# Attention of a fused two-block kernel: where a head pair's projections and sums of squares stand among its steps

## The reference, cut to what matters

```python
q = (rms_norm_2(q_lat, q_a_g) @ w_q_b).reshape(bsz, L, MLA_HEADS, MLA_QK)
kv = (rms_norm_2(kv_lat, kv_a_g) @ w_kv_b).reshape(bsz, L, MLA_HEADS, MLA_NOPE + MLA_V)
k_nope, v = jnp.split(kv, [MLA_NOPE], axis=-1)
k = jnp.concatenate([k_nope, jnp.broadcast_to(k_pe[:, :, None, :], (bsz, L, MLA_HEADS, MLA_ROPE))], axis=-1)
q = rms_norm_2(q, q_norm_g)
k = rms_norm_2(k, k_norm_g)
q = jnp.concatenate([q[..., :MLA_NOPE], apply_rope(q[..., MLA_NOPE:], cos, sin)], axis=-1)
k = jnp.concatenate([k[..., :MLA_NOPE], apply_rope(k[..., MLA_NOPE:], cos, sin)], axis=-1)
...
    sc = jnp.einsum('bqhd,bkhd->bhqk', q[:, s:e], k[:, :e]).astype(jnp.float32) * scale
    mask = jnp.arange(e)[None, :] <= jnp.arange(s, e)[:, None]
    p = jax.nn.softmax(jnp.where(mask, sc, -jnp.inf), axis=-1).astype(v.dtype)
    outs.append(jnp.einsum('bhqk,bkhd->bqhd', p, v[:, :e]))
o = jnp.concatenate(outs, axis=1).reshape(bsz, L, MLA_HEADS * MLA_V)
return o @ w_out
```

## Time and profile before

| | us |
|---|---|
| median of 3 runs | 2866.23 |
| lowest and highest run | 2855.94, 2868.21 |
| profiled execution, its own time | 2863.25 |
| its span | 2861.4 |
| TensorE busy in the span | 2715.2 (95%) |
| the eight pairs' steps | 2138.0 to 2460.0 |

### The profile page before, as it was taken

How to read it: one execution, slowest core, us unless ns; L and a number is a source line. 1 busy time by engine, 2 the same in 40 slices (tenths; PEclk the granted TensorE clock), 3 DMA queues, 4 the chain that set the end, 5 groups by cost and what they waited for, 6 DMA issues and landing times.

```text
span 2861.4 us, 35969 instructions
## 1 busy us (share of the span) xinstructions
PE 2715.2 (95%) x15144; PEld 2310.3 (81%) x15144; DVE 1189.6 (42%) x1641; ACT 976.4 (34%) x1479; POOL 925.5 (32%) x381
## 2 busy tenths in 40 slices
PE   6999999899999987999999999999979999999999
PEld 4777778677777777999888999999957777778887
DVE  6444441444444237666666331112344444421111
ACT  3333333323333333444334332223333333433222
POOL 3343344333434432222222333444320000244443
PEclk9999999999999998999999999999976677999999
DMA  3233333222333221211121222332210000133332
GB/s 122 90 107 90 100 98 89 75 91 83 113 91 98 91 74 45 60 54 59 52 59 53 76 87 90 89 92 87 77 52 8 15 8 15 60 94 92 94 96 89
DMA packets 61328, 215.65 MB, mean 75 GB/s; under 512 B 8176, under 2 KB 8560, under 8 KB 61168
## 3 DMA queue, kind: packets, MB, share of 16 engines
q1 hardware_dynamic: 57248, 202.05, 23.5%
q10 hardware_dynamic: 3920, 11.31, 1.2%
HBM read 211.24 MB, written 2.10 MB: 75 GB/s over the span
## 4 chain that ended last, share of the span: by engine, by line
PE 89%; DVE 6%; ACT 2%; issue 2%; DMA 0%; POOL 0%; SPq 0%; ACTq 0%; DVEq 0%
PE psum L357 73%; PE psum L954 1%; PE psum L892 1%; PE psum L920 1%; PE psum L451 1%; PE psum L461 1%; PE psum L896 1%; PE psum L644 1%; PE psum L918 1%; PE psum L956 1%; PE psum L647 1%; PE psum L937 1%; PE psum L599 1%; PE psum L369 1%; PE psum L658 0%
## 5 line engine op out<-in xcount | busy, mean ns | idle before, releaser
L337 POOL TENSOR_TENSOR sb_w_lo<-sb_w_raw,sb_w_hi 128x1024 fp32r<-128x1024 f32 x377 | 925.3, 2457 | 1913.8 <-ACT sb_w_hi L1070 1913.6
L357 PE MATMUL psum<-sb_h_hi,sb_w_hi 128*128 128x512 f32 (+1 forms) x2648 | 827.6, 354 | 48.0 <-DVE sb_h_lo L1510 33.9
L357 PE MATMUL psum<-sb_h_lo,sb_w_hi 128*128 128x512 f32 (+1 forms) x2648 | 799.6, 344 | 0.0
L357 PE MATMUL psum<-sb_h_hi,sb_w_lo 128*128 128x512 f32 (+1 forms) x2648 | 796.3, 343 | 0.0
L1070 ACT ACTIVATE sb_w_hi<-sb_w_raw 128x1024 fp32r<-128x1024 f32 x377 | 395.5, 1054 | 612.3 <-PE psum L357 461.6
L357 PEld LDWEIGHTS psum<-sb_h_hi,sb_w_hi 128*128 128x128 f32 x2648 | 464.7, 193 | 120.1 <-issue 39.9
L357 PEld LDWEIGHTS psum<-sb_h_lo,sb_w_hi 128*128 128x128 f32 x2648 | 463.0, 192 | 62.8 <-issue 7.6
L357 PEld LDWEIGHTS psum<-sb_h_hi,sb_w_lo 128*128 128x128 f32 x2648 | 462.2, 192 | 56.1
L357 PE MATMUL psum<-sb_mix_hi,sb_w_hi 128*128 128x264 f32 (+1 forms) x1424 | 418.3, 339 | 11.5 <-DVE sb_mix_lo L2224 5.8
L357 PE MATMUL psum<-sb_mix_lo,sb_w_hi 128*128 128x264 f32 (+1 forms) x1424 | 416.0, 338 | 0.0
L357 PE MATMUL psum<-sb_mix_hi,sb_w_lo 128*128 128x264 f32 (+1 forms) x1424 | 414.1, 337 | 0.0
(11 more groups left out here) (269 smaller groups left out, 2671.9 us busy)
## 6 DMA issues: line engine op xcount, KB each, us to landing
sb_w_raw<-in_weights SPq DMA_DIRECT2D x377, 512.0 KB, 3.6
sb_decay<-in_decay ACTq DMA_DIRECT2D x16, 640.0 KB, 3.8
sb_resid<-in_x SPq DMA_DIRECT2D x4, 512.0 KB, 9.1
out<-sb_resid SPq DMA_DIRECT2D x8, 256.0 KB, 2.1
sb_table<-in_rope_table ACTq DMA_DIRECT2D x1, 264.0 KB, 3.6
sb_s<-in_positions ACTq DMA_DIRECT2D x1, 256.0 KB, 8.8
sb_cols<-in_cols ACTq DMA_DIRECT2D x1, 158.5 KB, 4.3
sb_ones<-in_ones ACTq DMA_DIRECT2D x1, 64.0 KB, 5.6
```

The costliest lines, as they stand in the source:

```text
L337: e.tensor_tensor(g.w_lo[:, u % 4, :], g.w_raw[:, u % 2, :], g.w_hi[:, u % 4, :].bitcast(F32), ALU.subtract).then_inc(S["w_lo"], 1)
L357: mm = e.matmul(g.psum[0:m, at + b, 0:wd], w[:, slot, P * i:P * i + m], xs[:, tile, c:c + wd], start=first and n == 0, stop=last and n == 2)
```

## The change

- **Blocks.** `pe_pair_block` issues one block. Block 0 goes behind step 2, block 1 between scores and transpositions of step 4, and two blocks each into steps 5, 6 and 7, one ahead of the transpositions and one at the end.
- **Sums.** `pe_pair_totals` is cut into halves of a head and uses banks 2 and 3 alone: half 0 behind step 1, the next inside step 2, the other head's two inside and behind step 3. The second head waits until `dve_pair_mean` has read the first.
- **VectorE.** The second turn part goes to step 1 and the third to step 2, the mean comes in two halves (steps 2 and 3), Newton moves to steps 5, 5 and 6, the key products to steps 6 and 7; the finished pair's output to step 4; `dve_finish` goes behind the other pair work of its step.
- **ScalarE.** The square of the queries goes ahead of the exponential of step 7, the reciprocal root to step 4, the split to step 2, the output copy to step 3. A first split of the output projection moves from behind the steps into the last pair.
- **TensorE, other.** `pe_out_turn` goes from step 4 to step 2. The output projection's fillers stand singly at 21 places in the last two pairs, in units 0, 1 and 2; seven blocks of unit 3 take the place of seven of unit 2 behind the steps, then come four last blocks (they were three), then units 4 to 7 (they were 3 to 7).

The number of instructions of each kind stays the same, but for one more mean per pair at half the size.

```diff
+PAIR_BLOCKS = tuple((3 * h + n, n, h, n == 0, n == 2) for h in range(2) for n in range(3))
+PAIR_BLOCKS += ((6, 3, 2, True, False), (7, 4, 2, False, True))
+def pe_pair_block(g, e, pair, i):
+    u = U_PAIRS[pair]
+    if i == 0:
+        e.wait_ge(S["lat_lo"], 5)
+        e.wait_ge(S["w_lo"], u + 1)
+        if pair:
+            e.wait_ge(S["q_squared"], pair)
+            e.wait_ge(S["turn"], 2 * pair + 2)
+    if i == 3 and pair >= 3:
         e.wait_ge(S["mix3"], pair - 2)
+    if i == 6 and pair:
+        e.wait_ge(S["mean"], rs_qk(pair - 1))
...
+def pe_pair_totals(g, e, pair, h, half):
+    if half == 0:
+        if h == 0:
+            e.wait_ge(S["q_squared"], pair + 1)
+            e.wait_ge(S["k_squared"], pair + 1)
+        else:
+            e.wait_ge(S["qk_mean"], pair + 1)
...
+    bank = 2 + half
...
-MLA_BANKS = (0, 2, 4, 5)
-FILL = {ALL_STEPS - 11: [(0, range(0, 3))], ALL_STEPS - 10: [(0, range(3, 6))],
-        ALL_STEPS - 7: [(1, range(0, 2))], ALL_STEPS - 6: [(1, range(2, 6))],
-        ALL_STEPS - 2: [(0, range(6, 7)), (1, range(6, 7))]}
+MLA_BANKS = (0, 2, 3, 4, 5, 0, 2, 3)
+FILLERS = [(m, n) for m in range(3) for n in range(PAIRS - 2)] + [(m, PAIRS - 2) for m in range(3)]
+PLACES = [(NS * (PAIRS - 2) + n, at) for n, at in ((2, 1), (4, 0), (5, 0), (5, 1), (6, 0), (6, 1), (7, 0), (7, 1))]
+PLACES += [(NS * (PAIRS - 1) + n, at) for n in range(1, NS) for at in range(2) if (n, at) != (4, 1)]
...
         pe_scores(g, e, i)
+        if more and n == 2:
+            pe_pair_totals(g, e, pair + 1, 0, 1)
+        if more and n == 3:
+            pe_pair_totals(g, e, pair + 1, 1, 0)
+        if project and n >= 4:
+            pe_pair_block(g, e, pair + 2, (1, 2, 4, 6)[n - 4])
...
         if i >= 1:
             pe_turn_p(g, e, i - 1)
         if i >= 2:
             pe_times_v(g, e, i - 2)
-        if pair + 1 < PAIRS:
-            if n == 1:
-                pe_pair_totals(g, e, pair + 1, 0)
-            if n == 2:
-                pe_pair_totals(g, e, pair + 1, 1)
-        if pair and n == 4:
+        if more and n == 1:
+            pe_pair_totals(g, e, pair + 1, 0, 0)
+        if more and n == 3:
+            pe_pair_totals(g, e, pair + 1, 1, 1)
+        if project and n == 2:
+            pe_pair_block(g, e, pair + 2, 0)
+        if pair and n == 2:
             pe_out_turn(g, e, pair - 1)
-        if pair + 2 < PAIRS:
-            if n == 5:
-                pe_pair_queries(g, e, pair + 2, 0)
-            if n == 6:
-                pe_pair_queries(g, e, pair + 2, 1)
-                pe_pair_keys(g, e, pair + 2)
+        if project and n >= 5:
+            pe_pair_block(g, e, pair + 2, (3, 5, 7)[n - 5])
...
+    pe_mla_out(g, e, 3, range(0, 3))
     pe_times_v(g, e, ALL_STEPS - 1)
-    pe_mla_out(g, e, 2, range(0, 7))
+    pe_mla_out(g, e, 3, range(3, 7))
     pe_out_turn(g, e, PAIRS - 1)
...
+    for m in range(4):
+        pe_mla_out(g, e, m, range(7, 8))
+    for m in range(4, KT):
         pe_mla_out(g, e, m, range(8))
```

More of the change, by code:

```diff
@@ L964, in pe_out_turn @@
     if pair + 2 < PAIRS:
-        e.wait_ge(S["mean"], rs_qk(pair + 2))
+        e.wait_ge(S["turn"], 2 * (pair + 2) + 4)
     if pair:
@@ L1004, in pe_mla @@
     pe_v(g, e, 0)
-    pe_pair_queries(g, e, 0, 0)
-    pe_pair_queries(g, e, 0, 1)
-    pe_pair_keys(g, e, 0)
+    for k in range(8):
+        pe_pair_block(g, e, 0, k)
     pe_v(g, e, 1)
[L1009 to L1013, removed]
+    for h in range(2):
+        for half in range(2):
+            pe_pair_totals(g, e, 0, h, half)
+    for k in range(8):
+        pe_pair_block(g, e, 1, k)
     for i in range(ALL_STEPS):
         pair, n = divmod(i, NS)
+        more, project = pair + 1 < PAIRS, pair + 2 < PAIRS
         pe_scores(g, e, i)
+        if more and n == 2:
[4 more added lines that the diff above has]
+            pe_pair_block(g, e, pair + 2, (1, 2, 4, 6)[n - 4])
+        if (i, 0) in FILL:
+            m, k = FILL[i, 0]
+            pe_mla_out(g, e, m, [k])
         if i >= 1:
@@ L1364, in act_pair_q_squares @@
     if pair:
-        e.wait_ge(S["qk_total"], pair)
+        e.wait_ge(S["qk_total"], 2 * pair)
     e.activation(g.square[0:QK, :, 0:SEQ], g.psum[0:QK, 0:2, :],
@@ L1423, in act_mla @@
     act_split(g, e, U_PAIRS[1] + LEAD)
-    act_rsqrt(g, e, rs_qk(0), g.mean2[:, :], g.rinv2[0][:, :])
+    act_pair_rsqrt(g, e, 0)
     act_pair_q_squares(g, e, 1)
-    act_pair_keys(g, e, 1)
     for i in range(ALL_STEPS):
         pair, n = divmod(i, NS)
+        if pair + 2 < PAIRS and n == 7:
+            act_pair_q_squares(g, e, pair + 2)
         act_exp(g, e, i)
@@ L2121, in dve_pair_plain @@
     S = g.S
-    e.wait_ge(S["q_proj"], pair + 1)
     e.wait_ge(S["q_squared"], pair + 1)
@@ L2177, in dve_pair_newton, with dve_pair_keys @@
         e.scalar_tensor_tensor(y, t, 1.5, y, ALU.add, ALU.mult).then_inc(S["newton"], 1)
-def dve_pair_keys(g, e, pair):
+def dve_pair_keys(g, e, pair, part):
     S = g.S
@@ L2240, in dve_mla @@
         dve_top(g, e, i)
-        if n == 1 and pair:
-            dve_finish(g, e, pair - 1, 1)
-        if n == 5:
-            dve_finish(g, e, pair, 0)
-        if n == 6 and pair:
-            dve_pair_out(g, e, pair - 1)
         if pair + 1 < PAIRS:
```

140 lines of the change are left out of this document (73 added, 67 removed).

## The result

The changed kernel takes 2823.55 us, the median of four runs (2832.88, 2814.31, 2814.26, 2832.78), beside 2867.22 us for the kernel before in the same session. The ratio is 0.9849, with a 95% interval of 0.9817 to 0.9881: 1.5% faster. The forecast was 2855.0, with a range that began at 2826, so the change was faster, as forecast, and by three and a half times as much (43.7 us against 12 from the same median; the two profiled executions, 2863.25 and 2832.88, differ by 30.4 us where the prediction's sum is 8.2).

A forecast was written before the change was run, and what follows sets the result against it. TensorE's own work at two clock prices was taken as the bound, waits as the smaller part. Terms -11.4 - 4.2 + 4.5 + 0.4 - 2.4 + 3.3 + 1.6 = -8.2 us, from 2863.25 to 2855; range 2826 to 2880.

The forecast's parts named there:

- The bound and the prices: Pairs' steps: TensorE's own work bounds; 28.2 us a pair at full clock, plus 0.447 us per microsecond at half clock.
- The waits: TensorE's waits for other engines in pairs 1 to 6: from 2.5 to 0.6 us a pair, -11.4 us.
- The new wait behind the squares of the keys: First sums of a pair would wait for ScalarE's late key copy and square: 0.2 to 0.6 us a pair.
- The half clock: Pairs 1 to 6: time at the lower clock falls from 27.5 to 26 us a pair, -4.2 us for six.
- the three places where the clock might return: Within a pair: step 3, step 4 or step 7, after 19, 19 or 35 us, weighed 0.4, 0.2, 0.4.
- Rival 3: Clock returns only in step 7 without the run of blocks: 36 us at half clock a pair, 2887 us; chance 0.16.
- Rival 1's middle case: Spread blocks keep work dense, clock up for longer: 15 us at half clock in each pair, 2825 us; chance 0.14.
- The sums let it fall: Steps 1 to 3: the sums' thin work brings the clock down, some 5.5 us of full-clock work into the pair.
- Pair 0: First pair: half clock grows from 17 to 27 us, +4.5 us.
- The ends: Last pair's idle time 3.0 to 0.6 us, -2.4; behind the steps, wait ahead of unit 4 +3.3, clock fall +1.6.
- The page on the clock: Skill page's rule: removing idle gaps would keep the clock up; the prediction said the trace disagrees, TensorE being busy throughout.

The follow-up runs named there:

- e1: Changed kernel with its eight blocks put back to three behind step 5 and five behind step 6: 2873.94 us, ratio 1.0024 to before.
- e2: Changed kernel with 16 useless matmuls added per pair around the sums of squares in steps 1 to 3: 2804.21 us, ratio 0.9788 to before.
- f1: Changed kernel with blocks 0 to 2 among the sums in steps 2 and 3, other blocks, fillers, second sums and third turn part moved: 2791.66 us.
- e4: Changed kernel with VectorE's turn parts and ScalarE's square of the queries put back to their old places: 2875.13 us, ratio 1.0024 to before.
- g3: Changed kernel with only ScalarE's square of the queries put back behind step 7's exponential and copy: 2875.02 us, ratio 1.0015 to before.
- g4: Kernel before with only its eight blocks spread over steps 4 to 7: 2833.38 us, ratio 0.9878 to before.
- g1: Changed kernel with the sums of squares back behind steps 1 and 2, a whole head each: 2822.77 us, ratio 0.9841 to before.
- f4: Kernel before with 24 useless matmuls added per pair, twelve behind the first head's sums, twelve ahead of the second's: 2894.6 us, ratio 1.0091.
- e3: Changed kernel with 16 useless matmuls added per pair, eight each at the ends of steps 5 and 6: 2839.99 us, ratio 0.9903 to before.

## Why the prediction was wrong

The sign was right, and so was it that the waits and the time at the half clock are the two terms that move. How the clock's term moves was wrong, in size and in the reasons given, and it is the larger of the two. The time, 2823.55, lies 2.5 us under the range's lower end. Its steps in turn:

- **The bound and the prices: right.** Work at two prices and waits as the smaller part. The 28.2 us and the 0.447 us for each microsecond at the half clock give the mean length of the pair within 0.4 us in the kernel after and in e1, e2, f1, e4 and g3, at 3 to 41 us of half clock. The two terms as measured, -15.7 and -18.3, and 1.5 for the two blocks that moved into pair 6, come to -32.5, against -32.3.
- **The waits: too small.** From 2.5 to 0.6 us a pair was forecast, -11.4 for six; they fell to 0.15, so -15.7, my bound of "no wait at all". The new wait behind the squares of the keys that I charged at 0.2 to 0.6 us a pair came once, in pair 0.
- **The half clock: the step that failed.** "I weigh them 0.4, 0.2 and 0.4, which gives 26 us a pair against 27.5", with the three places where the clock might return. It returned in step 4 in all six pairs, the place that I gave 0.2, and 19 us had been the figure for it; measured were 20.5. The term was -4.2 us for six pairs and came to 0.447 x (163.8 - 122.9) = -18.3. (The weights and the figures 19, 19 and 35 give 25.4, not 26; that is worth 1.6 us in six pairs.) A mean over three places is also a value that none of them gives. And it is one level only: in the runs at 2814 us the granted clock of the whole kernel is 0.961 instead of 0.953, so 2 x 0.047 x 2831 - 2 x 0.039 x 2812 = 47 us less at the half clock, worth 21 us, beside 18.6 between the levels.
- **What the failure rested on.** I argued that without the run of five blocks the clock might return as late as step 7, with a weight of 0.4. g4 shows the opposite: with that run taken apart and nothing else moved, the clock returned 23 to 31 us into the pair, where it had returned after 34 to 35 in five pairs of six. e1 goes the other way. That the single blocks help because they stand where dense work was missing is my reading; g4 also loses waits. Rival 3, with 0.16, had the wrong sign for its cause. Rival 1's middle case (2825, with 15 us at the half clock) came nearest: the median lies between the level with 20.5 us a pair and one with some 13 (20.5 - 47/6, if all of it lies in those six pairs).
- **"The sums let it fall": not borne out.** The clock fell 5.7 us into the pair, where I had 5.5, but that agreement says little. In the kernel before it fell ahead of the sums in pairs 1, 2, 3 and 5, by 1.2 to 2.1 us. Window and timeline of before, pair 1, where a wait of 0.86 us ended at 2178.26:

```profile
2178.90:2180.16 1.26, 1.26 (x7) 1.03 (x6) 1.22 (x2) 1.13 (x2) 0.00 (x0) 0.50 0.00 0
```

```profile
2180.16 1.24 PE L892 MATMUL psum<-sb_ksq,sb_ones 64*128 64x264 f32 x2
```

In e1 it fell 4 us ahead of them; in the kernel after and in f1 it fell just behind the first head's first half. g1 packs the sums again and takes as long as the kernel after. What brings the clock down is therefore open; what the runs show is which orders bring it back sooner.

- **Pair 0**: +4.5 forecast, +1.5 measured (38.0 us). Its stretch at the half clock was 24 us, I took 27; and its idle time fell from 4.1 to 2.7 us, which I left out.
- **The ends: right.** Idle time in the last pair 0.55 us (0.6 forecast); ahead of unit 4 3.39 us (3.6 forecast), and behind it 3.4 us at the half clock, 1.5 us (1.6 forecast). The wait for the low output part stayed at 1.41 us.
- **The page on the clock.** In the kernel after TensorE idles 0.15 us in a pair of 37.5 and its clock is down for 20.4 us at a stretch, busy in all 20.40. The Trainium skill, page "TensorE: Matmul & The Clock Gate", section "HAM oscillation — how this bites in real kernels", puts a clock that falls in the middle of a kernel down to gaps in which the engine idles. The measurement decides: here gaps are not needed for it to stay down, nor for it to fall. A part for short waits isn't excluded: in pair 1 of the kernel before, in e1, e4 and g3 one stands at or ahead of the fall, and in g3 5.4 us of waits go with 123 us more at the half clock; but f1 idles 4.2 us with 21 us at the half clock. In e2 the clock stays up in the pair shown when matmuls of 128 rows and 240 columns stand behind those of the sums.

What stays open: what brings the clock down in a pair, since no run is without the sums; whether the spread blocks bring it back by their place or in part by the wait that they cover; why 0.7 us more waiting in a pair (g3) doubles the time at the half clock; what chooses between the two levels of one kernel; and whether f1's gain comes from the blocks beside the sums alone or in part from the sums' own places. That last point wasn't tried apart.

## What to carry to other kernels

Where a loop's rows show two granted clocks, price its work at both, and read for each turn of the loop when the clock falls and when it returns. Then try the densest matmuls that can be moved singly at and behind the place where it falls, measure it (f4 shows that it can fail), and judge an edit on another engine by whether it shifts the clock's return and not by the wait it removes alone. Don't average over places of return: give each its own time and chance.

## What the runs showed of the hardware

- TensorE's clock falls and stays at its lower level with the engine busy throughout: 20.40 of 20.40 us after, 34.20 of 34.20 in e1, 40.88 of 40.90 in e4. Busy time alone doesn't tell the level; where the dense matmuls stand among the others changes it (123 us at the half clock after, 20 in e2, 21 in f1).
- Ninety-six more matmuls in six pairs made those pairs 34.7 us shorter (e2); sixteen a pair at another place made them 4.2 us longer (e3), and twenty-four a pair in the kernel before 20 us longer (f4).
- A loop can settle into turns of the same length within 0.2 us, and into different ones by run: six turns of 37.4 to 37.5 us after, five of 47.7 to 47.8 in g3. The levels of the whole time are 19 us apart after, 37 us in e4 and 40 us in g3.
